# A chunked linear-attention scan, unrolled, with its second half of one chunk issued ahead of the first half of the next

## What is computed

```python
def gla_chunked(q, k, v, log_a):             # GLA_CHUNK = 64 tokens, 4 heads, key width 64, value width 128
    bc = jnp.cumsum(to_chunks(log_a), axis=-2)
    def step(S, inp):
        q_c, k_c, v_c, b_c = inp
        o_inter = jnp.einsum('bhcd,bhde->bhce', q_c * jnp.exp(b_c), S)
        ...
        o_intra = jnp.einsum('bhij,bhje->bhie', scores, v_c)
        S = (S * jnp.exp(b_last[:, :, 0, :])[..., None]
             + jnp.einsum('bhcd,bhce->bhde', k_c * jnp.exp(b_last - b_c), v_c))
        return S, o_inter + o_intra
...
    o_f = gla_chunked(q_h, k_h, v_h, heads(log_a[:, :, 0], GLA_DK))
    o_b = flip(gla_chunked(flip(q_h), flip(k_h), flip(v_h), flip(heads(log_a[:, :, 1], GLA_DK))))
    o = (o_f + o_b).transpose(0, 2, 1, 3)
    o = rms_norm(o, norm_w) * jax.nn.silu(g.reshape(B, T, GLA_HEADS, GLA_DV))
```

## Time and profile before

| | us |
|---|---|
| median of 3 runs (3117.67 to 3118.09) | 3117.79 |
| the profiled execution's own time | 3118.62 |
| its span in the trace | 3116.8 |

### The profile page before, as it was taken

How to read it: one execution, slowest core, us unless ns; L and a number is a source line. 1 busy time by engine, 2 the same in 40 slices (tenths; PEclk the granted TensorE clock), 3 DMA queues, 4 the chain that set the end, 5 groups by cost and what they waited for, 6 DMA issues and landing times. The chain is left out here.

```text
span 3116.8 us, 48973 instructions
## 1 busy us (share of the span) xinstructions
PE 2917.9 (94%) x18460; PEld 2396.5 (77%) x18460; DVE 1782.3 (57%) x2599; ACT 1063.6 (34%) x1664; POOL 1280.3 (41%) x649
## 2 busy tenths in 40 slices
PE   7999989999999999999999999979869967999997
PEld 5766778888888888888888888857669955788775
DVE  1354369874777777067777777753846554433115
ACT  3366333343333333321211211245433444433223
POOL 3622333554444444444444444433334322344442
PEclk9999999999999999999999999989989988999998
DMA  3211222444445544655555555522652101222231
GB/s 114 88 61 55 84 86 91 146 134 130 166 165 192 193 166 167 232 175 191 203 196 183 189 197 196 176 80 76 215 160 52 29 14 54 74 94 99 97 101 68
DMA packets 173745, 404.23 MB, mean 130 GB/s; under 512 B 55344, under 2 KB 55472, under 8 KB 172336
## 3 DMA queue, kind: packets, MB, share of 16 engines
q1 hardware_dynamic: 173616, 402.39, 39.2%
HBM read 318.45 MB, written 83.89 MB: 129 GB/s over the span
## 5 line engine op out<-in xcount | busy, mean ns | idle before, releaser
L158 POOL TENSOR_TENSOR weights_low<-weights_raw,weights_high 128x1024 fp32r<-128x1024 f32 x435 | 1128.8, 2595 | 1584.5 <-ACT weights_high L150 1584.5
L150 ACT ACTIVATE weights_high<-weights_raw 128x1024 fp32r<-128x1024 f32 x435 | 460.7, 1059 | 1633.0 <-PE psum L258 1617.0
L256 PE MATMUL psum<-expert_in_high,weights_high 128*128 128x512 f32 x1152 | 458.9, 398 | 8.4 <-DVE expert_in_low L351 4.8
L257 PE MATMUL psum<-expert_in_low,weights_high 128*128 128x512 f32 x1152 | 450.1, 391 | 0.0
L258 PE MATMUL psum<-expert_in_high,weights_low 128*128 128x512 f32 x1152 | 450.0, 391 | 0.0
L256 PE MATMUL psum<-coefficients_high,weights_high 128*128 128x512 f32 x1024 | 399.3, 390 | 5.9 <-DVE coefficients_low L1219 4.2
L257 PE MATMUL psum<-coefficients_low,weights_high 128*128 128x512 f32 x1024 | 398.9, 390 | 0.0
L258 PE MATMUL psum<-coefficients_high,weights_low 128*128 128x512 f32 x1024 | 398.8, 389 | 0.0
L1219 DVE TENSOR_TENSOR coefficients_low<-activation_in,coefficients_high 128x512 fp32r<-128x512 f32 x128 | 354.8, 2772 | 4.4
L256 PEld LDWEIGHTS psum<-expert_in_high,weights_high 128*128 128x128 f32 x1152 | 217.3, 189 | 56.6 <-issue 8.7
L258 PEld LDWEIGHTS psum<-expert_in_high,weights_low 128*128 128x128 f32 x1152 | 217.0, 188 | 45.6
(11 more groups left out here) (380 smaller groups left out, 4661.1 us busy)
## 6 DMA issues: line engine op xcount, KB each, us to landing
weights_raw<-in_weights SPq DMA_DIRECT2D x437, 512.0 KB, 3.5
expert_activations<-expert_activation SPq DMA_DIRECT2D x128, 256.0 KB, 4.0
coefficient_table<-table_stage SPq DMA_DIRECT2D x8, 4096.0 KB, 13.2
table_group<-coefficient_table SPq DMA_DIRECT2D x128, 256.0 KB, 4.1
activation_in<-expert_activations SPq DMA_DIRECT2D x128, 256.0 KB, 3.6
chunk_b_k_v<-scan_vectors SPq DMA_DIRECT2D x8, 768.0 KB, 6.1
scan_vectors<-scan_stage SPq DMA_DIRECT2D x4, 1280.0 KB, 6.7
scan_vectors<-scan_stage SPq DMA_DIRECT2D x4, 1024.0 KB, 6.1
```

The lines of the kernel that those rows point to most:

```text
L150: act.activation(d.hi[:, m % SPLIT, :], d.raw[:, m % RAW, :], ACT.Copy).then_inc(d.high, 1)
L158: pool.tensor_tensor(d.lo[:, m % SPLIT, :], d.raw[:, m % RAW, :], d.hi[:, m % SPLIT, :].bitcast(F32), ALU.subtract).then_inc(d.split, 1)
L256: pe.matmul(acc, w[0][:, cols], x[0], start=start, stop=False)
L257: pe.matmul(acc, w[0][:, cols], x[1], start=False, stop=False)
```

## The change

Four things are changed:

- `gla_scan` is written out chunk by chunk instead of a hardware loop, and PE's order becomes: front 0 and front 1 of chunk 0, then in each chunk back 0, front 0 of the next chunk, back 1, front 1 of the next chunk. DVE and ACT follow the same order. In chunk 0 the product with the (zero) state is left out, after chunk 7 the state product and its update.
- `bd` gets a second buffer. POOL waits for the output product of two chunks before.
- `gla_v` is stored so that PE can turn the values of a chunk straight from it: `vx`, its copies (L2684) and their semaphores go. The convolution of v now works in the rows of `gla_z` that are no longer read, the SiLU writes the new layout, and the reversed copy at the end of `rwkv_scan` has the shape 8 x 64 in place of 512 columns.
- The gate's load and its SiLU move from `gla_scan` to `rwkv_output`, the SiLU behind ACT's last exponential there.

```diff
-                for t in (bd, pb, S):
+                for t in (bd, pb):
...
-                with pool.Fori(0, NCH) as i:
+                for i in range(NCH):
                     for g in range(2):
-                        pool.wait_ge(banks[g][3].made, i + 1)
+                        if i > 1:
+                            banks[g][2].full(pool, i - 2, "o")
...
-                                pool.tensor_copy(bd[r, dst, half(g), r], src[r, half(g), bass.ds(i * C, C)]).then_inc(built[g], 1)
+                                pool.tensor_copy(bd[r, i % 2, dst, half(g), r], src[r, half(g), tokens(i)]).then_inc(built[g], 1)
...
+                for g in range(2):
+                    front(0, g)
+                for i in range(NCH):
                     for g in range(2):
+                        back(i, g)
+                        if i + 1 < NCH:
+                            front(i + 1, g)
...
-                        act.activation(vx[:, half(g), :].rearrange("p u (h t) -> p (u h) t", h=2),
-                                       v[:, g, :, bass.ds(i * C, C)], ACT.Copy).then_inc(vbuilt[g], 1)
...
+                    for g in range(2):
+                        o_out(i, g)
+                        if i + 1 < NCH:
+                            turned(i + 1, g)
-                act.wait_ge(gate_in, 16)
-                act.activation(gg[:, :, :], gg[:, :, :], ACT.Silu)
...
+                    for g in range(2):
+                        state(i, g)
+                        masks(i + 1, g)
...
-            dve.tensor_copy(self.v[:, 1, n, ::-1], self.v[:, 0, n, :])
+            dve.tensor_copy(self.v_head(1, n)[:, ::-1, ::-1], self.v_head(0, n))
```

More of the change, by code:

```diff
@@ L2648, in _ @@
                         pe.sem_inc(b.made, 1)
-                pe.wait_ge(zeroed, 3)
-                with pe.Fori(0, NCH) as i:
+                pe.wait_ge(zeroed, 2)
+                for g in range(2):
+                    front(0, g)
+                for i in range(NCH):
                     for g in range(2):
[L2652 to L2675, removed]
-                        for u in range(H):
-                            mm = pe.matmul(st.ps[:, u * P:(u + 1) * P], kv[:, g, 0, u, :], kv[:, g, 1, u, :], start=True, stop=True)
-                        mm.then_inc(st.made, 1)
@@ L2695, in _, with turned, o_out @@
-                act.wait_ge(gate_in, 16)
-                act.activation(gg[:, :, :], gg[:, :, :], ACT.Silu)
+                def turned(i, g):
+                    tr = banks[g][1]
+                    tr.full(act, i, "turned")
+                    act.activation(kv[:, g, :, :, :].rearrange("p a u t -> p (a u t)"), tr.ps, ACT.Copy).then_inc(tr.read, 1)
+                def o_out(i, g):
+                    o = banks[g][2]
+                    o.full(act, i, "o")
+                    act.activation(ob[:, g, :, tokens(i)], o.ps[:, 0:2 * H * C].rearrange("p (h t) -> p h t", t=C),
+                                   ACT.Copy).then_inc(o.read, 1)
@@ L2698, in _, with masks @@
+                for g in range(2):
+                    turned(0, g)
+                for i in range(NCH):
+                    for g in range(2):
+                        o_out(i, g)
+                        if i + 1 < NCH:
+                            turned(i + 1, g)
             @block.vector
             def _(dve):
+                def masks(i, g):
+                    sc = banks[g][0]
+                    sc.full(dve, i, "scores")
+                    for hh in range(2):
+                        r = slice(hh * C, hh * C + C)
+                        m = consts("upper_eq")[r, None, :].to_broadcast([C, H, C])
+                        ins = dve.tensor_tensor(pb[r, half(g), r], sc.ps[r, 0:H * C].rearrange("p (u t) -> p u t", u=H),
+                                                m, ALU.mult)
+                    ins.then_inc(sc.read, 1)
@@ new lines, in state @@
+                def state(i, g):
+                    st = banks[g][3]
+                    st.full(dve, i, "S")
+                    src = st.ps[:, 0:H * P].rearrange("p (u t) -> p u t", u=H)
+                    decay = ends[:, half(g), i:i + 1].to_broadcast([P, H, P])
+                    if i == 0:
+                        dve.tensor_tensor(S[:, half(g), :], src, decay, ALU.mult).then_inc(st.read, 1)
+                    else:
+                        dve.tensor_tensor(S[:, half(g), :], src, S[:, half(g), :], ALU.add).then_inc(chain[g], 1)
+                        dve.wait_ge(chain[g], i)
+                        dve.tensor_tensor(S[:, half(g), :], S[:, half(g), :], decay, ALU.mult).then_inc(st.read, 1)
@@ L2702, in _ @@
                         dve.sem_inc(b.read, 1)
-                dve.wait_ge(zeroed, 3)
-                with dve.Fori(0, NCH) as i:
+                dve.wait_ge(zeroed, 2)
+                for g in range(2):
+                    masks(0, g)
+                for i in range(NCH - 1):
                     for g in range(2):
[L2706 to L2714, removed]
-                        st = banks[g][3]
-                        st.full(dve, i, "S")
-                        src = st.ps[:, 0:H * P].rearrange("p (u t) -> p u t", u=H)
-                        dve.tensor_tensor(S[:, half(g), :], src, S[:, half(g), :], ALU.add).then_inc(chain[g], 1)
-                        dve.wait_ge(chain[g], i + 1)
-                        dve.tensor_tensor(S[:, half(g), :], S[:, half(g), :],
-                                          ends[:, half(g), bass.ds(i, 1)].to_broadcast([P, H, P]), ALU.mult).then_inc(st.read, 1)
+                        state(i, g)
+                        masks(i + 1, g)
 def gla_output(nc, k, ob, gg, out):
```

80 lines of the change are left out of this document (54 added, 26 removed).

## The result

| | before | after |
|---|---|---|
| median (5 runs each) | 3118.09 us (3117.67 to 3120.55) | 3102.51 us (3101.11 to 3104.37) |
| profiled execution, span | 3118.62, 3116.8 | 3101.11, 3099.3 |
| the scan's Block | 55.42 | 39.75 |
| time per chunk at full clock | 5.81 | 4.35 |
| granted clock, mean | 0.973 | 0.973 |

The ratio is 0.9947, 95% interval 0.9934 to 0.9959: 0.5% faster, forecast 3102.8.

What follows compares the result with a forecast made beforehand. PE was taken as the bound: scan's Block 4.33 + 36.05 + 0.76 + 0.26 = 41.4 us, 14.0 less; `gla_output` 1.0 less; 3118.62 less 15.0 is 3103.6, median 0.8 below: 3102.8 us, range 3099.8 to 3106.8.

Steps and rivals of the forecast that it cites:

- PE bounds the steady chunk at 4.34 us: Scan's steady chunks: PE's two fronts and two backs set the time, 4.34 us; DVE, ACT and POOL all stay below.
- Why it was at 5.81: Old scan loop: 4.34 us PE work plus 1.47 us waiting per turn, blamed on a round trip over ACT and POOL.
- PE's passes and the tail, 36.05 + 0.76 + 0.26 = 37.07: Scan's Block: 36.05 us of PE passes, 0.76 to the last output copy's end, 0.26 step to the next Block.
- The slow clock in it, 6.1 us long: Scan's start: PE at half clock for 6.1 us after the first pass, adding 3.05 us, bound +-1.0.
- Head 4.33: Start of the scan's Block: after changed zeroing on POOL, +0.42 us, PE's first pass comes 4.33 us in.
- Gate 0: Gate's table load and SiLU moved into `rwkv_output`: cost nothing under DVE's work; 3.2 us without that cover.
- Layout of v 0: Reversed copy of v ending `rwkv_scan`, now 8 x 64: costs 0; +1.4 us if it ran at half rate.
- `gla_output` gains 1.0: Eight PE passes in `gla_output`: a shorter PE pause may keep the clock up, gaining 0 to 2.05 us; 1.0 taken.
- POOL's copies: Rival: POOL becomes the scan's bound if each copy takes its 542 ns maximum, 3.4 us more, 3106.2 us; chance 0.10.
- late code: Rival: the unrolled scan code arrives late, 0.78 us for each of seven chunks, 5.5 us, 3108.3 us; chance 0.04.
- The pipeline formed: Rival was that it doesn't form: scan turns keep 5.81 us, only 2.8 us gained, 3115.0 us; chance 0.05.
- A sign of failure that came up: Whole kernel: the prediction fails if something outside the scan's Block moves by more than 1 us.

Runs made afterwards that it cites:

- first profile: The changed kernel's first profiled execution, nothing altered: 3101.11 us, the scan's Block 39.75 us.
- second profile: The changed kernel run and profiled once more, nothing altered: median 3102.81 us, ratio 0.9949, the scan's Block 40.64 us.
- the twelve unread products: Changed kernel plus 12 PE matmuls nobody reads, nine ending `rwkv_output`, three heading the scan: 3099.85 us, in another set of runs 3100.68.
- the four profiles named above: Four variants of the changed kernel: twelve unread matmuls (3099.85 us); one block-diagonal buffer, new order (3120.19) and old order (3107.80); POOL's copies done twice (3107.14).

## Why the prediction was right, step by step

- *PE bounds the steady chunk at 4.34 us*: right, 4.35, no hole, the others wait for PE.
- *Why it was at 5.81*: here a step of mine failed although the number held. I wrote that the wait was PE "plus a round trip over ACT and POOL at its head, which a loop that issues front and back of one chunk together can't cover". The old order, unrolled, with two buffers and values turned directly, issues them just so and runs at 4.53. What stood at the head was the copy of the values (0.58) and the single buffer (0.47 to 0.73, by what stands beside it), as the earlier trace rows named them; the loop, with what else differs there, adds 0.23, and the round trip that only the new order hides is 0.18. My sum took PE as the bound with all parts together, so it didn't ask which part brings it there.
- *PE's passes and the tail, 36.05 + 0.76 + 0.26 = 37.07*: 2517.84 to 2553.84, 36.00.
- *The slow clock in it, 6.1 us long*: 4.1 in the first profile, 5.9 in the second. That is 1.0 us of Block time less in the one, which is all but 0.07 of the difference, and 0.1 in the other; it was given +-1.0. That the clock is what takes these 2 to 3 us is shown by the twelve unread products.
- *Head 4.33*: 3.75. The zeroings are as long as forecast, but the first copy follows 0.07 us behind them (0.34 in the loop) and the first pass 1.42 behind that (1.69).
- *The Block 41.4*: 39.75 and 40.64.
- *Gate 0*: right, and 3.2 us when it is bare, as priced. *Layout of v 0*: right, 1.43 us against 1.42; the bound of +1.4 wasn't needed.
- *`gla_output` gains 1.0*: 13.32 to 13.11, 0.2, and 12.77 in the second profile. PE's pause was 2.7 us, as worked out, but the clock fell about when the products began, and they ran at 5.40 us (5.65 before). The guess lay between two cases of which this was the unfavourable one; in the four profiles named above the clock held and this Block was 1.6 us shorter (11.53).
- *Rivals*: POOL's copies reached 418 ns, not 542, and never held PE up in the steady chunks; what makes them a bound is sixteen of them. No chunk shows late code. The pipeline formed, and with one buffer it would have ended worse than the rival that I priced for that (7.14 per chunk against 5.81). The clock didn't stay low.
- *A sign of failure that came up*: the prediction was to fail if something outside the Block moved by more than 1 us. In the first profile two things did, the start of `rwkv_output` (2.86 earlier) and its length (1.38 more). The other profiles show such differences between like code as well, so this sign was drawn too tightly to tell anything.

The medians: 3102.8 forecast, 3102.5 and 3102.8 measured. Errors that partly cancel: the Block was 1.65 better in the profile, `gla_output` 0.8 worse, and what lay ahead of the scan another 1.5 better (2.86 - 1.38). So the profiled execution came out 2.5 us below the 3103.6 worked out for it, while the median lay 1.4 above its profile and not 0.8 below. That the two meet within 0.3 us is luck; the medians of the kernel before, taken beside each set of runs, went from 3116.8 to 3118.7 themselves.

## What to carry to other kernels

A pipelined order and a second buffer are one change: here the buffer alone gave 0.47 to 0.73 us per chunk, the order without it cost 1.9, and the order on top of the buffer gave 0.18. Before crediting an order, remove the named waits one by one; most of the gain came from not copying the values and from the buffer. An engine's table load and activation at a Block's end cost their full 3.2 us there and nothing under another engine's tail.

## What was not expected of the hardware

The instructions of `rwkv_output`, the same but for the gate and the unread products, took 18.07 to 18.25 us in nine profiles and 19.35 to 19.62 in five. Near its start the granted clock stood at 0.50 for 3.4 us in each of the nine and for 6.8 us in each of the five. After the scan's first pass it stayed there for 4.1 to 6.7 us, in the eleven profiles without unread products. One profile of a kernel this size therefore gives the length of such a Block within 1 to 2 us only, and its place less well, unless TensorE's clock is at the same level in both; time per chunk at full clock doesn't suffer from that, and medians do less.
